# A hybrid decoder layer on one core: jobs of 144 rows, and the recurrence's first steps moved into the attention

## The reference

```python
# the recurrence, per head: bc = cumsum(log f), f the gate
inter = einsum('bhtk,bhkv->bhtv', q_ * exp(b_), state)
rel = where(causal, b_[:, :, :, None, :] - b_[:, :, None, :, :], -inf)
att = einsum('bhtk,bhtsk,bhsk->bhts', q_, exp(rel), k_)
intra = einsum('bhts,bhsv->bhtv', att, v_)
...
attn = rmsnorm(attn, attn_out_g[l])            # mean of squares over the heads' 512 columns
...
# the experts, per block of rows of one expert e
hid = dot(xblk, w1[e]) + b1[e]
glu, lin = minimum(hid[:, 0::2], 7), clip(hid[:, 1::2], -7, 7)
act = glu * sigmoid(1.702 * glu) * (lin + 1)
yb = dot(act, w2[e]) + b2[e]
```

## Time and profile before

| what | value |
|---|---|
| median of 3 runs | 2070.32 us (2068.22 to 2071.92) |
| the profiled execution, its own time | 2069.33 us |
| its span, first to last instruction | 2067.7 us |
| mean granted TensorE clock | 0.982 |
| PE busy | 1965.6 us, 95% |
| DVE busy | 1580.4 us, 76% |
| ACT busy | 1342.1 us, 65% |
| POOL busy | 667.3 us, 32% |
| HBM traffic over the span | 245 GB/s |

### The profile page before, as it was taken

How to read it: one execution, slowest core, us unless ns; L and a number is a source line. 1 busy time by engine, 2 the same in 40 slices (tenths; PEclk the granted TensorE clock), 3 DMA queues, 4 the chain that set the end, 5 groups by cost and what they waited for, 6 DMA issues and landing times.

```text
span 2067.7 us, 39657 instructions
## 1 busy us (share of the span) xinstructions
PE 1965.6 (95%) x11170; PEld 1683.2 (81%) x11171; DVE 1580.4 (76%) x2202; ACT 1342.1 (65%) x1931; POOL 667.3 (32%) x758
## 2 busy tenths in 40 slices
PE   7999998879987999999999999999999999999995
PEld 6888877877765888889788897979897888979884
DVE  5334256875678788989888898889898888988886
ACT  5231156663437586877768777787778687777865
POOL 3100001321244142524325244344244252443423
PEclk9999999999978999999999999999999999999998
DMA  5323121113357898989899898999898998989987
GB/s 194 72 82 102 56 78 42 42 49 111 123 170 284 283 315 290 351 274 356 288 314 326 280 370 275 333 314 370 275 359 292 309 334 281 364 268 337 317 286 249
DMA packets 267760, 507.35 MB, mean 245 GB/s; under 512 B 39148, under 2 KB 44268, under 8 KB 267320
## 3 DMA queue, kind: packets, MB, share of 16 engines
q1 hardware_dynamic: 244042, 453.98, 63.8%
q0 software_dynamic: 23664, 52.67, 9.6%
HBM read 463.09 MB, written 43.53 MB: 245 GB/s over the span
## 4 chain that ended last, share of the span: by engine, by line
PE 64%; issue 1%; DMA 1%; ACT 1%; POOL 1%; DVE 1%; POOLq 0%; ACTq 0%; DVEq 0%
PE ps L1225 17%; PE ps L732 11%; PE ps L734 11%; PE ps L733 10%; PE ps L1227 7%; PE ps L1265 3%; PE ps L1266 3%; PE ps L1117 2%; PE ps L1198 1%; ACT whi L1591 0%; DMA raw<-acc_d,icur 0%; PE ps L1189 0%; DVE wlo L2277 0%; DMA acc_d<-y,icur 0%; ACT y L1622 0%
## 5 line engine op out<-in xcount | busy, mean ns | idle before, releaser
L2277 DVE TENSOR_TENSOR wlo<-raw,whi 128x1024 fp32r<-128x1024 f32 x764 | 912.8, 1219 | 110.1 <-ACT whi L1591 106.0
L1591 ACT ACTIVATE whi<-raw 128x1024 fp32r<-128x1024 f32 x764 | 830.4, 1117 | 134.3 <-PE ps L1227 93.0
L1225 PE MATMUL ps<-xT,whi 128*128 128x320 f32 x1920 | 504.6, 349 | 6.3 <-DVE wlo L2277 5.8
L1227 PE MATMUL ps<-xT,wlo 128*128 128x160 f32 x1920 | 456.0, 238 | 0.0
L1225 PEld LDWEIGHTS ps<-xT,whi 128*128 128x128 f32 x1920 | 363.2, 189 | 10.0 <-DVE wlo L2277 6.2
L1227 PEld LDWEIGHTS ps<-xT,wlo 128*128 128x128 f32 x1920 | 369.1, 192 | 0.5
L2627 POOL DMA_INDIRECT acc_d<-y,icur x93 | 161.2, 1733 | 443.7 <-ACT y L1625 258.5
L732 PE MATMUL ps<-whi,xT 128*128 128x512 f32 x544 | 218.1, 401 | 3.2 <-DVE wlo L2133 3.2
L732 PE MATMUL ps<-whi,aT 128*128 128x512 f32 x512 | 212.9, 416 | 3.0 <-DVE aTl L2333 3.0
L734 PE MATMUL ps<-whi,xT 128*128 128x512 f32 x544 | 213.2, 392 | 0.0
L733 PE MATMUL ps<-wlo,xT 128*128 128x512 f32 x544 | 212.8, 391 | 0.0
(11 more groups left out here) (348 smaller groups left out, 3553.5 us busy)
## 6 DMA issues: line engine op xcount, KB each, us to landing
raw<-in_w SPq DMA_DIRECT2D x768, 512.0 KB, 9.9
raw<-in_w_in SPq DMA_DIRECT2D x16, 512.0 KB, 5.9
xs<-in_x SPq DMA_DIRECT2D x8, 512.0 KB, 10.5
raw<-in_w_out SPq DMA_DIRECT2D x8, 512.0 KB, 3.8
mix<-in_x SPq DMA_DIRECT2D x8, 512.0 KB, 3.7
h_d<-h SPq DMA_DIRECT2D x8, 512.0 KB, 2.7
acc_d<-mix SPq DMA_DIRECT2D x8, 512.0 KB, 4.4
raw<-acc_d SPq DMA_DIRECT2D x8, 512.0 KB, 8.4
```

What stands on the lines that cost most here:

```text
L1225: pe.matmul(o2, wh[:, a, cols], xT2[:, :, k, 0:JOB_T], start=q == 0 and a == 0, stop=False, skip_group_check=True)
L1227: m = pe.matmul(o, wl[:, a, cols], xT2[:, 0, k, 0:JOB_T], start=False, stop=q == QUARTERS - 1 and a == 1, skip_group_check=True)
L1591: act.activation(parted(slot(whis, s)), paired(raw_slot(s), s), ACT.Copy).then_inc(split_hi, 1)
L2277: dve.tensor_tensor(parted(slot(wlos, s)), paired(raw_slot(s), s), parted(slot(whis, s).bitcast(F32)), ALU.subtract).then_inc(split_lo, 1)
```

## The change

Jobs of 129 to 144 rows run `job(j, 2, NARROW)`, with 144 for 160 as the number of rows that are moved on TensorE, ScalarE and VectorE; other jobs run as before. GpSimd and SP do for them what they did. In the attention, two of VectorE's differences come ahead of the last block's heads, GpSimd's wait for the last scores alone and not for the last heads, six of the eight head squares come one by one behind a block's exponentials, and the other two at steps 3 and 4 of the recurrence. Head 0's keys are loaded ahead of unit 7's weights, level(0, 0) runs ahead of diagonal(0), and the four tables are set up at step 4 of GpSimd's loop.

```diff
+NARROW = 144
+EARLY_ARGS = 2
 # SP
             for n in range(2, 8):
+                if n == 7:
+                    for i in range(len(hg_out)):
+                        sp.wait_ge(hg_out[i], hg_stores(i, NT))
+                    sp.wait_ge(keys_out, 16)
+                    sp.dma_start(hkey[:, :, :], keys_d[:, :, 0:P]).then_inc(hkey_in, 16)
                 for q in range(QUARTERS):
                     raw_free(n, q)
                     weights(n, q)
-            for i in range(len(hg_out)):
-                sp.wait_ge(hg_out[i], hg_stores(i, NT))
-            sp.wait_ge(keys_out, 16)
-            sp.dma_start(hkey[:, :, :], keys_d[:, :, 0:P]).then_inc(hkey_in, 16)
             sp.wait_ge(heads_out, 2 * NT)
 # TensorE
-            pe.wait_ge(heads_out, 2 * NT)
...
+            level(0, 0)
+            pe.wait_ge(heads_out, 2 * NT)
             diagonal(0)
-            level(0, 0)
...
-            def job(j, blocks):
+            def job(j, blocks, width=JOB_T):
...
-                        o = ps[:, bank, 0:JOB_T]
-                        o2 = ps[:, bank, 0:2 * JOB_T].rearrange("p (h n) -> p h n", h=2)
+                        o = ps[:, bank, 0:width]
+                        o2 = ps[:, bank, 0:2 * JOB_T].rearrange("p (h n) -> p h n", h=2)[:, :, 0:width]
...
-                            pe.matmul(o2, wh[:, a, cols], xT2[:, :, k, 0:JOB_T], start=q == 0 and a == 0, stop=False,
+                            pe.matmul(o2, wh[:, a, cols], xT2[:, :, k, 0:width], start=q == 0 and a == 0, stop=False,
...
-                            m = pe.matmul(o, wl[:, a, cols], xT2[:, 0, k, 0:JOB_T], start=False,
+                            m = pe.matmul(o, wl[:, a, cols], xT2[:, 0, k, 0:width], start=False,
...
                             with pe.If(left < P + 1):
                                 job(j, 1)
                             with pe.Else():
-                                job(j, 2)
+                                with pe.If(left < NARROW + 1):
+                                    job(j, 2, NARROW)
+                                with pe.Else():
+                                    job(j, 2)
 # ScalarE (its job's sigmoid and aT_wide take 0:width too, and its branch is TensorE's)
+            def square_heads(t):
+
+                act.wait_ge(heads_out, 2 * t + 2)
+                square(t, 0, attT[1][:, 0:4, :].rearrange("p a b -> p (a b)"))
             for n in range(NT):
                 for kv in range(NKV):
                     probs_copied(2 * n + kv)
                 if n + 1 < NT:
                     for kv in range(NKV):
                         exps(2 * n + 2 + kv)
+                if n >= 2:
+                    square_heads(n - 2)
                 if n in SPLIT_AT:
                     split(6, SPLIT_AT[n])
-            for t in range(NT):
-                act.wait_ge(heads_out, 2 * t + 2)
-                square(t, 0, attT[1][:, 0:4, :].rearrange("p a b -> p (a b)"))
...
+                if s in (3, 4):
+                    square_heads(NT - 5 + s)
 # VectorE (sum_up, hidden_wide, activate_wide and aT_wide take 0:width too, and its branch is TensorE's)
                 if n + 1 < NT:
                     find_max(2 * n + 3)
+                if n == NT - 1:
+                    dve.wait_ge(scored, 2 * NT)
+                    for s in range(EARLY_ARGS):
+                        args(s)
                 heads_scaled(2 * n)
...
                     if L == 0:
                         dve.wait_ge(diag_done, hd + 1)
+                        if hd == 1:
+                            dve.wait_ge(msq, NT)
...
-                if s < STEPS * HH:
+                if EARLY_ARGS <= s < STEPS * HH:
                     args(s)
...
-                return dve.tensor_reduce(o, ps[:, b:b + 2, 0:2 * JOB_T].rearrange("p i (h n) -> p i n h", h=2), AX, ALU.add)
+                halves = ps[:, b:b + 2, 0:2 * JOB_T].rearrange("p i (h n) -> p i n h", h=2)
+                return dve.tensor_reduce(o, halves[:, :, 0:width, :], AX, ALU.add)
 # GpSimd
-            pool.wait_ge(heads_out, 2 * NT)
-            iota(iotaE[:, :], [[1, NE]], 0)
-            iota(iotaR[:, 0:P], [[1, P]], 0, 1)
-            iota(iotaR[:, P:2 * P], [[0, 4], [1, HALF]], 0, P + 1)
-            iota(tok[:, :], [[P, NT]], 1, -T)
             pool.wait_ge(sums_set, HH)
             pool.wait_ge(shift_in, 16)
+            pool.wait_ge(scored, 2 * NT)
             for s in range(STEPS * HH):
                 hd, L = divmod(s, STEPS)
+                if s == RING:
+                    pool.wait_ge(heads_out, 2 * NT)
+                    iota(iotaE[:, :], [[1, NE]], 0)
+                    iota(iotaR[:, 0:P], [[1, P]], 0, 1)
+                    iota(iotaR[:, P:2 * P], [[0, 4], [1, HALF]], 0, P + 1)
+                    iota(tok[:, :], [[P, NT]], 1, -T)
...
             pool.wait_ge(bias_turned, 1)
+            pool.memset(aT2[:, :, P:2 * P].bitcast(F32), 0.0).then_inc(y_zero, 1)
             pool.memset(y[:, 1, :], 0.0).then_inc(y_zero, 1)
...
-            pool.wait_ge(y_zero, 1)
+            pool.wait_ge(y_zero, 2)
```

More of the change, by code:

```diff
@@ L1430, in square @@
                 squares[0] += 1
[L1432 removed]
+            def square_heads(t):
                 act.wait_ge(heads_out, 2 * t + 2)
                 square(t, 0, attT[1][:, 0:4, :].rearrange("p a b -> p (a b)"))
+            for n in range(NT):
+                for kv in range(NKV):
+                    probs_copied(2 * n + kv)
+                if n + 1 < NT:
+                    for kv in range(NKV):
+                        exps(2 * n + 2 + kv)
+                if n >= 2:
+                    square_heads(n - 2)
+                if n in SPLIT_AT:
+                    split(6, SPLIT_AT[n])
             def outs(hd):
@@ L1591, in jsplit, with sigmoid @@
                 act.activation(parted(slot(whis, s)), paired(raw_slot(s), s), ACT.Copy).then_inc(split_hi, 1)
-            def sigmoid(j, c, blocks):
+            def sigmoid(j, c, blocks, width):
                 if c > 0:
@@ L1626, in y_out, with step @@
                                    scale=gcur[0:2 * HALF, 1:2]).then_inc(y_set[1], 1)
-            def step(j, blocks, s):
+            def step(j, blocks, s, width):
                 if UNIT_END.get(s - 1, 0) == 4:
@@ L1633, in step @@
                 if UNIT_END.get(s - 1, 4) < 4:
-                    sigmoid(j, UNIT_END[s - 1], blocks)
+                    sigmoid(j, UNIT_END[s - 1], blocks, width)
                 jsplit(j, s + AHEAD_HI)
@@ L1694, in job @@
                     for s in range(LAST_ACT, NS):
-                        step(j, blocks, s)
+                        step(j, blocks, s, width)
                     for b in range(blocks):
@@ L1722, in _ @@
                             with act.Else():
-                                job(j, 2)
+                                with act.If(left < NARROW + 1):
+                                    job(j, 2, NARROW)
+                                with act.Else():
+                                    job(j, 2)
         @block.vector
@@ L2383, in last_step, with job @@
                 if blocks == 2 and s in WIDE_TURN_AT:
-                    aT_wide(j, WIDE_TURN_AT[s])
+                    aT_wide(j, WIDE_TURN_AT[s], width)
                 if s in NORM_AT:
                     norm_tile(s)
-            def job(j, blocks):
+            def job(j, blocks, width=JOB_T):
                 for s in range(LAST_DVE):
-                    step(j, blocks, s)
+                    step(j, blocks, s, width)
                 with dve.If(j + 1 > total - 1):
@@ L2394, in job @@
                     for s in range(LAST_DVE, NS):
-                        last_step(j, blocks, s)
+                        last_step(j, blocks, s, width)
                     add_rows(j, 5, blocks).then_inc(rows_set, 1)
@@ L2429, in _ @@
                             with dve.Else():
-                                job(j, 2)
+                                with dve.If(left < NARROW + 1):
+                                    job(j, 2, NARROW)
+                                with dve.Else():
+                                    job(j, 2)
         @block.gpsimd
```

88 lines of the change are left out of this document (43 added, 45 removed).

## The result

The changed kernel takes 2422.15 us (2411.57 to 2423.95, four runs), the kernel before beside it 2071.12: a ratio of 1.1688 (95% interval 1.1672 to 1.1704), 351 us slower, where 2047 was predicted. Its profiled span is 2422.3 us.

What follows compares the result with a forecast made beforehand. TensorE was taken to bound the jobs. Term 1's 22.0 us plus 1.0 net of terms 2 and 3 gave 23.0 off 2069.3, 2046.3, or 2047 at the runs' median; range 2036 to 2056, likeliest case 2043 to 2052.

Steps and rivals of the forecast that it cites:

- term 1: Wide jobs' matmuls: a pair falls from 260 to about 247 ns, saving 22.0 us over 13 jobs.
- Rival (d): Start of each wide job: second branch and longer program hold TensorE up; at 2.0 us a job 2077; 3 in 100.
- columns alone: Wide jobs' pairs: time goes by columns only, saving 20 ns a pair, 33 us in all, 2036; 7 in 100.
- the floor under the narrower half: Wide jobs' 160-column products: the weight load sets about 110 ns, so narrowing them to 144 gains nothing.
- Term 2: Start of the recurrence: keys loaded early and differences moved ahead let diagonal(0) end 5.0 us earlier.
- term 3: Attention: moved squares cost 2.5 us and POOL's differences beside the last maxima 1.9 us.
- the next difference: Recurrence: POOL's difference at level 4, made while VectorE waits for the diagonal, lifts the net gain to about 1.0 us.
- (b): Wide jobs: weight loads bound both halves, so the change does nothing there, 2069; 5 in 100.
- (c): Wide jobs: a feeder such as VectorE becomes the bound; if half the gain is lost, 2058; 8 in 100.

Runs made afterwards that it cites:

- two_bodies_144: Changed kernel without the third body, its one wide body at 144 columns for all 15 wide jobs, rows past 144 left out: 2043.21 us, ratio 0.9867.
- the shared form: Changed kernel, third body on TensorE alone, wide jobs' last 8 steps once behind both arms: 2183.29 us; with the 160-column body in the middle, 2204.39.

## Why the prediction was wrong

**The failed step** is in term 1: "The test of the new width is one more branch ... I price it at 0; without that cover it would cost 15 times the branch." The branch does cost nothing (2070.80 with the test alone, on ScalarE). What was priced at nothing is the third body behind it: 391 more instructions in TensorE's loop, about 135 each in ScalarE's and VectorE's. Shown: with it taken out the loss is gone (2069.91); with it on any one engine it costs 146, 315 or 229 us; bodies that are never executed still cost 337 (2407.32), with ScalarE's and VectorE's packets as many as in the changed kernel; and on ScalarE alone 90 unused instructions cost 339 us where 40 cost nothing. Each time the instruction packets rise with the time.

**Rival (d)** named the place and half of the mechanism, "the second branch and the longer program hold TensorE up at the start of each wide job", and was mis-sized. It had 2 us a job; the changed kernel lost 2422.2 - 2046.8 = 375 us, 25 for each wide job and the narrow one beside it. What spoke against it, that TensorE passes today's border without a gap, could not: that border lies in a loop that stays loaded. The row which could have spoken is on the page of before: 32 and 22 packets for the whole program, and none in the pair of the earlier trace rows. It says that the loop was held, and nothing about how much longer it could get.

**Term 1's own size was right.** A pair went from 260 to 244 ns (predicted 247, with columns alone 240), a job gave 1.78 us (1.69), 13 jobs 23.1 (22.0). The weight loads of two_bodies_144 say where the difference lies: the distance under the wider product fell by 15 ns (150 to 135, predicted 13), the other by 2 (110 to 108). So the floor under the narrower half held nearly, and the slope is steeper than taken: 15 / 32 = 0.47 ns a column for 0.41.

**Term 2 was right in the trace, term 3 in its mechanisms, and too large.** From the last heads to the diagonal on VectorE: 9.95 us before (342.56 to 352.51), 4.95 after (347.04 to 351.99), the 5.0 of term 2. The attention's end came 4.5 us later against 2.5 + 1.9 = 4.4, but that agreement is luck, since 1.0 of the 4.5 stood there before the first moved step. The change's own 3.5 are, to 0.1 us, three waits for copies, 0.6 longer in each of the two blocks with a split (0.73 to 1.33 and 1.34, predicted 0.8 each) and 0.7 in the last pair (0.88 to 1.59, predicted 0.8), and 1.5 at the last maxima (predicted 1.9), where the two small steps take 0.96 and 1.03 us, as the prediction put them. Net that is 1.5 us (5.0 - 3.5), predicted 0.6 up to there and 1.0 with the next difference; on the clock of the whole kernel, ratio 0.9998, it can't be seen.

**Rivals (b) and (c)** did not come: at 144 columns with two bodies the kernel kept 26.7 us of the 15 x 128 x 16 ns = 31 us that the pairs gave, so the feeders cost 4 at the most.

## What to carry to other kernels

A specialised copy of a loop's body is not free because its branch is: look at the page's instruction queues, which in a loop that stays loaded move nothing, and count the instructions of the loop on every engine, not of the copy that runs. If a copy is wanted, give it to the engine that gains from it alone (here TensorE, since the others had time for 160 columns), and try the bodies in the other order (114 us better with whole bodies, 21 us worse in the shared form) and the loop at another place in the program: third_on_pe_pad and third_on_pe_pad160, the change's narrow products on TensorE with 112 or 160 unused slots ahead of its loop, keep all rows, beat both kernels and repeat, at 2053.79 and 2055.61 us. That gain hangs on the loop's place, and a later edit ahead of the loop can take it away.

## What the hardware showed that was not expected

- ScalarE's loop has a sharp edge, measured at one place of the loop: about 316 instructions 2069.46 us, about 366 instructions 2408.99 us, and 2385.07 with about 404. Longer was not dearer once it was over the edge.
- TensorE fetched nothing again with an unexecuted body in the middle of its loop (33 packets) and in every pair with a rarely executed one at its end (146), while ScalarE and VectorE fetched again for a body that they only jumped over (338 packets).
- Moving TensorE's loop by 112 slots in the program was worth 139 us (2192.64 to 2053.79).
- Waits of 9.05 and 10.64 us on TensorE were followed by 6.3 us at a granted clock of 0.55 and 8.1 us at 0.66.
